# The embedding product moved to the start of a two-block network, with a new order of the queues around both places

## The reference

```python
h = rms_norm(x, norm_mix_pre);  z = h @ w_in            # nine splits: zq .. zu, zv, ga, gb
mix = merged(z) @ w_out;        x = x + rms_norm(mix, norm_mix_post)
h2 = rms_norm(x, norm_ffn_pre); ff = (silu(h2 @ w_gate) * (h2 @ w_up)) @ w_down
x = x + rms_norm(ff, norm_ffn_post)
x = x + (p @ w_ple) * sigmoid(x @ w_ple_gate)           # p: 256 x 256, w_ple: 256 x 1024
```

## Time and profile before

| What | us |
| --- | --- |
| median of 3 runs (1141.11 to 1141.41) | 1141.21 |
| the profiled execution | 1141.63 |
| its span, from first to last instruction | 1139.6 |
| PE busy | 1128.8 (99%) |
| DVE busy | 847.6 (74%) |
| ACT busy | 542.6 (48%) |
| first matmul of stage zu | 11.50 |
| first matmul of stage zv | 24.16 |

### The profile page before, as it was taken

One profiled execution on the slowest core, in us unless ns is written; L12 is line 12 of the kernel. 1 busy time (PEld: TensorE's weight loads), 2 busy tenths in 40 slices (PEclk: granted clock), 3 DMA queues, 4 the chain that ended last, 5 costly groups with the idle time before them and its releaser, 6 DMA issues.

```text
span 1139.6 us, 14114 instructions
## 1 busy us (share of the span) xinstructions
PE 1128.8 (99%) x5874; PEld 965.8 (85%) x5874; DVE 847.6 (74%) x951; ACT 542.6 (48%) x545; POOL 29.2 (3%) x51
## 2 busy tenths in 40 slices
PE   9999999999999999999999999999999999999997
PEld 7998998888888888888888888889988888888886
DVE  6789879977766768567676767579976866767685
ACT  6646556633753444355644444353333435444431
POOL 1000000000100000000000000000001000000000
PEclk9999999999999999999999999999999999999999
DMA  7854554447557787544467777558763664886760
GB/s 268 318 214 152 183 215 138 163 153 307 214 206 301 253 309 264 221 171 146 151 233 284 272 281 297 200 211 302 273 233 118 231 249 159 308 303 254 305 223 37
DMA packets 37534, 259.81 MB, mean 228 GB/s; under 512 B 4192, under 2 KB 4704, under 8 KB 6880
## 3 DMA queue, kind: packets, MB, share of 16 engines
q1 hardware_dynamic: 35856, 251.84, 59.7%
q0 software_dynamic: 1616, 7.08, 1.8%
HBM read 257.86 MB, written 1.05 MB: 227 GB/s over the span
## 4 chain that ended last, share of the span: by engine, by line
PE 96%; issue 1%; DVE 1%; ACT 1%; DMA 1%; SPq 0%; POOL 0%; POOLq 0%; DVEq 0%; ACTq 0%
PE pair L460 47%; PE pair L523 23%; PE pair L486 10%; PE pair L539 4%; PE tp L587 3%; PE tp L669 3%; PE tp L885 1%; PE pair L823 1%; PE tp L696 1%; DMA raw<-stream 1%; PE tp L861 1%; PE tp L610 0%; PE tp L649 0%; PE pair L728 0%; PE pair L722 0%
## 5 line engine op out<-in xcount | busy, mean ns | idle before, releaser
L1324 DVE TENSOR_TENSOR w_lo<-raw,w_hi 128x2048 fp32r<-128x2048 f32 x180 | 409.0, 2288 | 78.8 <-ACT w_hi L911 78.3
L911 ACT ACTIVATE w_hi<-raw 128x2048 fp32r<-128x2048 f32 x180 | 344.2, 1916 | 225.6 <-DMA raw<-stream 125.0
L460 PE MATMUL pair<-w_hi,ht_lo 128*128 128x512 f32 x800 | 316.3, 395 | 0.0
L460 PE MATMUL pair<-w_lo,ht_hi 128*128 128x512 f32 x800 | 311.9, 390 | 0.0
L460 PE MATMUL pair<-w_hi,ht_hi 128*128 128x512 f32 x800 | 311.6, 389 | 0.0
L460 PEld LDWEIGHTS pair<-w_lo,ht_hi 128*128 128x128 f32 x800 | 150.2, 188 | 31.7
L460 PEld LDWEIGHTS pair<-w_hi,ht_lo 128*128 128x128 f32 x800 | 150.3, 188 | 30.0 <-DVE ht_lo L1384 0.5
L460 PEld LDWEIGHTS pair<-w_hi,ht_hi 128*128 128x128 f32 x800 | 150.4, 188 | 29.5
L1333 DVE SCALAR_TENSOR_TENSOR raw<-raw,crow 128x1024 f32<-128x1024 f32 x112 | 132.3, 1219 | 0.9 <-DMA raw<-stream 0.9
L523 PE MATMUL pair<-w_hi,gt_lo 128*128 128x512 f32 x272 | 107.0, 393 | 0.3 <-DVE gt_lo L1400 0.3
L523 PE MATMUL pair<-w_lo,gt_hi 128*128 128x512 f32 x272 | 106.0, 390 | 0.0
(11 more groups left out here) (258 smaller groups left out, 1316.3 us busy)
## 6 DMA issues: line engine op xcount, KB each, us to landing
raw<-stream SPq DMA_DIRECT2D x237, 1024.0 KB, 4.9
xres<-x SPq DMA_DIRECT2D x2, 512.0 KB, 5.0
raw<-stream SPq DMA_DIRECT2D x4, 256.0 KB, 7.2
prow<-rows POOLq DMA_DIRECT2D x1, 1024.0 KB, 8.5
xres<-x POOLq DMA_DIRECT2D x2, 512.0 KB, 5.3
dt<-decay POOLq DMA_DIRECT2D x1, 1024.0 KB, 9.5
csr<-dft POOLq DMA_DIRECT2D x1, 768.0 KB, 6.2
sgw<-sg_wT POOLq DMA_DIRECT2D x1, 512.0 KB, 5.3
```

The lines of the kernel that those rows point to most:

```text
L460: mm = pe.matmul(pair[use % 2][:, t, :], a[:, 4 * c + k, t * P:(t + 1) * P], b[:, w % WS, k * 512:(k + 1) * 512], start=(c == 0 and k == 0 ...
L911: sc.activation(w_hi[:, w % WS, :], raw[:, n % RAW, :], ACT.Copy).then_inc(hi_done, 1)
L1324: v.tensor_tensor(w_lo[:, w % WS, :], raw[:, n % RAW, :], whi32[:, w % WS, :], ALU.subtract).then_inc(raw_done, 1)
```

## The change

Stage `ple` becomes the first of the stream. SP asks for p first, then for chunk 0 (now ple) and chunk 1 (now the first of zu) in four pieces each, and for chunk 2. x's two tiles, the identity and the table `col` are issued by ACT, with a semaphore each for the last two (`idn_in`, `col_in`). p lies in another place in memory, `plex` at the end, and the memory set aside for the descriptors of GpSimd's DMAs is given as 8192 bytes. The product goes in four quarters `embed(0..3)` into three free PSUM banks and one more, in front of and behind the first transposes; `keep_warm` goes, and WARM is 12. ACT's four copies are spread over the start. Every tick in the mixer moves by one, as do the numbers of the `ada` ticks there. Behind the mixer, PE has no `embed()`, and ACT and DVE have another order of ticks and norms. Cut to its core:

```diff
-WARM = 18
+WARM = 12
 RAW = 3
 WS = 4
 GROUPS = FT // 2
-STAGES = [("zu", 2), ("zv", 2), ("qa", 2), ("fa", 2), ("ba", 2), ("zi", 4), ("zg", 4),
+STAGES = [("ple", 1), ("zu", 2), ("zv", 2), ("qa", 2), ("fa", 2), ("ba", 2), ("zi", 4), ("zg", 4),
...
-FINE = 2
+FINE = 3
...
-        praw = sb("praw", 193.25, [P, 2, S])
-        pt = [sb("pt_hi", 195.25, [P, 2, S], F32R), sb("pt_lo", 197.25, [P, 2, S], F32R)]
+        praw = sb("praw", 112, [P, 2, S])
+        pt = [sb("pt_hi", 114, [P, 2, S], F32R), sb("pt_lo", 116, [P, 2, S], F32R)]
...
+        def embedding(t, half):
+
+            if t == 0:
+                return pair[1][:, half, :]
+            return tp[BANKS - 1][:] if half else pair[0][:, 1, :]
...
-            sp.dma_start(xres[:, 0, :], x[:, 0, :]).then_inc(x_in[0], 16)
-            sp.dma_start(idn[:], ident).then_inc(small_in, 16)
-            sp.dma_start(xres[:, 1, :], x[:, 1, :]).then_inc(x_in[1], 16)
-            sp.dma_start(col[:], cols).then_inc(small_in, 16)
+            def piece(n, q, sem):
+                part = slice(q * 512, (q + 1) * 512)
+                sp.dma_start(raw[:, n, part], stream[n][:, part]).then_inc(sem[q], 16)
+
+            sp.dma_start(praw[:], pT).then_inc(p_in, 16)
+            piece(0, 0, first_in)
+            piece(0, 1, first_in)
+            piece(0, 2, first_in)
+            piece(0, 3, first_in)
             for q in range(PIECES):
-                sp.dma_start(raw[:, 0, q * 512:(q + 1) * 512], stream[0][:, q * 512:(q + 1) * 512]).then_inc(first_in[q], 16)
-            for n in range(1, RAW):
-                sp.dma_start(raw[:, n, :], stream[n]).then_inc(landed[n], 16)
+                piece(1, q, next_in)
+            sp.dma_start(raw[:, 2, :], stream[2]).then_inc(landed[2], 16)
...
-            pool.wait_ge(merged, 2)
-            pool.dma_start(praw[:], pT).then_inc(p_in, 16)
...
+            def embed(q):
+
+                k, half = q // 2, q % 2
+                part = slice(q * 512, (q + 1) * 512)
+                for t in range(TT):
+                    out = embedding(t, half)
+                    tk = slice(t * P, (t + 1) * P)
+                    if t == 0:
+                        pe.wait_ge(hi_done, q + 1)
+                    pe.matmul(out, pt[0][:, k, tk], w_hi[:, 0, part], start=(k == 0), stop=False)
+                    if t == 0:
+                        pe.wait_ge(pt_done, 1)
+                    pe.matmul(out, pt[1][:, k, tk], w_hi[:, 0, part], start=False, stop=False)
+                    if t == 0:
+                        pe.wait_ge(raw_done, q + 1)
+                    mm = pe.matmul(out, pt[0][:, k, tk], w_lo[:, 0, part], start=False, stop=(k == 1))
+                if k == 1:
+                    mm.then_inc(ple_done, 1)
...
-            pe.wait_ge(small_in, 32)
+            def last_tile():
+                pe.wait_ge(ple_read, 2)
+                first_tile(1, 1, xn_done, 2)
+
+            pe.wait_ge(pt_hi, 1)
+            embed(0)
+            embed(1)
+            pe.wait_ge(idn_in, 16)
             first_tile(0, 0, xn_half, 1)
-            keep_warm(8)
-            first_part(0, 0, after={0: next_halves})
-            first_part(0, 1, after={1: lambda: first_tile(1, 1, xn_done, 2)})
+            embed(2)
+            embed(3)
+            pe.matmul(tp[1][:, 0:16], ones[:], ones[:, 0:16], start=True, stop=True).then_inc(w_used, 1)
+            first_part(0, 0, after={1: next_halves})
+            pe.wait_ge(ple_read, 1)
+            first_part(0, 1, after={3: last_tile})
             first_part(1, 0)
             first_part(1, 1)
+            pe.wait_ge(ple_read, 4)
...
-            embed()
...
+            act.dma_start(xres[:, 0, :], x[:, 0, :]).then_inc(x_in[0], 16)
+            act.dma_start(idn[:], ident).then_inc(idn_in, 16)
+            act.dma_start(col[:], cols).then_inc(col_in, 16)
+            act.dma_start(xres[:, 1, :], x[:, 1, :]).then_inc(x_in[1], 16)
...
+            def embedded(t, half):
+                act.wait_ge(ple_done, half + 1)
+                sc.activation(plex[:, t, half * 512:(half + 1) * 512], embedding(t, half), ACT.Copy).then_inc(ple_read, 1)
+
+            act.wait_ge(p_in, 16)
+            sc.activation(pt[0][:], praw[:], ACT.Copy).then_inc(pt_hi, 1)
+            hi_piece(0, 0)
             norm_squares(RQ["norm0"], 0, 0)
-            norm_squares(RQ["norm0"] + 1, 1, 0)
-            for q in range(2):
+            for q in range(1, PIECES):
                 hi_piece(0, q)
             norm_hi("norm0", 0, 0)
-            for q in range(2, PIECES):
-                hi_piece(0, q)
+            norm_squares(RQ["norm0"] + 1, 1, 0)
+            hi_piece(1, 0)
+            embedded(1, 0)
+            for q in range(1, PIECES):
+                hi_piece(1, q)
             first_scaled(0)
             norm_hi("norm0", 1, 0)
+            embedded(1, 1)
             for q in range(PIECES):
-                hi_piece(1, q)
+                hi_piece(2, q)
             norm_hi("norm0", 0, 1)
             first_scaled(1)
             norm_hi("norm0", 1, 1)
-            for w in range(2, WS):
-                split_hi(w)
+            embedded(0, 0)
+            embedded(0, 1)
+            split_hi(3)
+            tick(0)
             act.wait_ge(lb_e, 1)
             sc.activation(lbt[:, 1, :], lbt[:, 0, :], ACT.Exp).then_inc(lb_e, 1)
-            tick(0)
-            pair_ready(1)
+            tick(1)
...
             post_squares(RQ["mix"], 0, w + 3, USE["wout"], 3)
             tick(w)
             norm_squares(RQ["mix"] + 1, 0, 1)
-            act.wait_ge(p_in, 16)
-            sc.activation(pt[0][:], praw[:], ACT.Copy).then_inc(pt_hi, 1)
             tick(w + 1)
             for half in range(2):
                 norm_scaled("norm1", 0, colv("ffn_pre", 0, 8), None, hb[:, tile_job("norm1", 0, half) % 2, :], half)
                 norm_hi("norm1", 0, half)
+            tick(w + 2)
             post_squares(RQ["mix"] + 2, 1, w + 3, USE["wout"], 3)
-            embedded(0)
-            tick(w + 2)
             tick(w + 3)
             norm_squares(RQ["mix"] + 3, 1, 2)
-            for n in range(1, 4):
-                embedded(n)
-            tick(W0["ple"])
             norm_his("norm1", 1, colv("ffn_pre", 0, 8))
...
+            dve.wait_ge(pt_hi, 1)
+            v.tensor_tensor(pt[1][:], praw[:], as_f32(pt[0][:]), ALU.subtract).then_inc(pt_done, 1)
+            lo_piece(0, 0)
+            mean(RQ["norm0"])
+            lo_piece(0, 1)
+            dve.wait_ge(rstd_done, RQ["norm0"] + 1)
             first_norm(0, 0, xn_half)
             first_norm(0, 1, xn_done)
-            dve.wait_ge(small_in, 32)
+            lo_piece(0, 2)
+            dve.wait_ge(col_in, 16)
+            first_scaled(0)
+            lo_piece(0, 3)
+            norm_lo("norm0", 0, 0)
             mean(RQ["norm0"] + 1)
-            first_scaled(0)
+            lo_piece(1, 0)
             dve.wait_ge(rstd_done, RQ["norm0"] + 2)
             first_norm(1, 0, xn_half)
-            lo_piece(0, 0)
-            norm_lo("norm0", 0, 0)
             for q in range(1, PIECES):
-                lo_piece(0, q)
+                lo_piece(1, q)
             first_norm(1, 1, xn_done)
             norm_lo("norm0", 1, 0)
             first_scaled(1)
-            lo_piece(1, 0)
+            lo_piece(2, 0)
             norm_lo("norm0", 0, 1)
             for q in range(1, PIECES):
-                lo_piece(1, q)
+                lo_piece(2, q)
...
             post(RQ["mix"], 0, USE["wout"], prow[:, 0, :])
             mean(RQ["mix"] + 1)
-            dve.wait_ge(pt_hi, 1)
-            v.tensor_tensor(pt[1][:], praw[:], as_f32(pt[0][:]), ALU.subtract).then_inc(pt_done, 1)
             scale_norm(RQ["mix"] + 1, 0)
             tick(w)
             tick(w + 1)
             norm_lo("norm1", 0, 0)
             norm_lo("norm1", 0, 1)
+            tick(w + 2)
             dve.wait_ge(x_again[1], 16)
             post(RQ["mix"] + 2, 1, USE["wout"], prow[:, 0, :])
-            tick(w + 2)
+            tick(w + 3)
             mean(RQ["mix"] + 3)
-            tick(w + 3)
             scale_norm(RQ["mix"] + 3, 1)
-            tick(W0["ple"])
             norm_jobs("norm1", 1, colv("ffn_pre", 0, 8))
```

More of the change, by code:

```diff
@@ L127, in plan_psum @@
              ("offb", 2, "off_copied"), ("pvb", 2, "pv_read"), ("ta", 4, "split"),
-             ("tm", 4, "split"), ("norm1", 2, "norm"), ("ple", 4, "ple_read"), ("norm1b", 2, "norm"),
+             ("tm", 4, "split"), ("norm1", 4, "norm"),
              ("h0", GROUPS, "split"), ("tx", 4, "split"),
@@ L159, in tile_job @@
         return JOB[name] + 2 * half + t
-    return (JOB[name + "b"] if name in ("norm1", "norm2") and t else JOB[name] + 2 * t) + half
+    return (JOB[name + "b"] if name == "norm2" and t else JOB[name] + 2 * t) + half
 PIECES = 4
-FINE = 2
+FINE = 3
 def pieces_done(n):
@@ L282, in program @@
         first_in = [sem(f"first_in{q}") for q in range(PIECES)]
+        next_in = [sem(f"next_in{q}") for q in range(PIECES)]
```

(45 more changed lines are left out.)

30 lines of the change are left out of this document (14 added, 16 removed).

## The result

| | before | changed |
| --- | --- | --- |
| median, us | 1141.4 (1141.11 to 1141.54, 5 runs) | 1147.88 (1146.44 to 1147.95, 5 runs) |
| the profiled execution | 1141.63 | 1146.62 |
| its span | 1139.6 | 1144.4 |
| first matmul of zu | 11.50 | 15.14 |
| first matmul of zv | 24.16 | 30.86 |

The changed kernel is slower: ratio 1.0052, 95% interval 1.0041 to 1.0063. The prediction (1144.0, range to 1147.0) had the sign right and the size too small; the median lies 0.9 above its range. The single times stand apart in two groups: 1146.44 and 1146.62, then 1147.88, 1147.90 and 1147.95. The profile is of the lower group.

A forecast was written before the change was run, and what follows sets the result against it. PE was taken as the bound, holding 96% of the time. Start +4.9 and boundary -2.1 sum to +2.8; the profiled execution (1141.63) gives 1144.4, the median 0.4 lower, 1144.0, range 1139.6 to 1147.0.

The forecast's parts named there:

- Landings at the start: Estimated DMA landings: p 4.3, x's first tile 5.4, chunk 0's quarters 5.5, 6.8, 8.2, 9.2; 2 us either way possible.
- the term for the start: Start of the kernel: zv begins at 29.1 instead of 24.2, +4.9, range +3.9 to +6.
- Step 2 and 3: Start: PE through embedding, transposes and matmul on ones at 13.0; zu's first product at 13.6 instead of 11.50.
- step 4: ACT from 12.9 to chunk 3: 10.4 of work and 1.5 of waiting; chunk 3 starts there at 24.8.
- the wait of 1.6 for a low part: PE, through its work at 27.5, waits until 29.1 for DVE's low part of chunk 3 before zv.
- x's tile late: Rival at the start: x shares the rate, lands at 7.5 instead of 5.4, all slides by 1.5: 1145.5; chance 0.10.
- The sentence on landings 1 us later: Start: with every landing 1 us later, zv would start at 30.1 instead of 29.1.
- the case of the slow clock: Rival at the start: the embedding runs at 1.2 GHz, 4.8 more, 3.4 on the path: 1147.4; chance 0.05.
- The boundary: Behind the mixer: removing 5.57 of PE work gives -2.1, after waits of 0.8, 0.4 and 2.3; bounds 0 and -4.8.
- The rule weighed: At the start, two issuing queues share the same 16 DMA engines, so x's tile shares the rate; only issue time saved.
- The rival "faster": PE's idling before 11.5 takes the embedding whole; start costs 0 to 0.5, boundary gives 2.1 to 4.8: 1138; chance 0.10.
- the bound with no other limit: Start term if ACT and DVE were no limit: PE's own work from 6.2, about 18.4, making +0.5.

The follow-up runs named there:

- the two profiles named above: Changed kernel with 18 matmuls on ones (1146.62 to 1148.22), and changed kernel with ACT's last two embedding copies behind chunk 3's split (1146.54).
- one queue: Changed kernel with x's two tiles, the identity and the columns table issued by SP between chunk 0's quarters, nothing by ACT: 1146.02, ratio 1.0039.
- both: Changed kernel with SP alone loading x's first tile ahead of p, lists reordered, 16 matmuls on ones, and post and scaling ahead of chunks at the boundary: 1142.21.
- supply of quarters: The version called both, with identity and `col` issued by ACT, and x's second tile and its squares behind chunk 0's quarters: 1142.62, ratio 1.0011.
- the run with only this part: Kernel before without the embedding product and its weights, with the changed kernel's boundary order and descriptor memory: 1140.47, ratio 0.9991.
- The reordered one: Changed kernel with ACT's squares and DVE's post of tile 1 ahead of chunk w+2, mean and scaling ahead of tick(w+3): 1146.5, ratio 1.0042.

## Why the prediction was wrong

**What failed first is the part "Landings at the start": the term for the start was +4.9 and measured +6.7 at zv, +6.8 at the boundary.** I took p at 4.3, x's first tile at 5.4 and chunk 0's quarters at 5.5, 6.8 and so on. Measured: p 6.0, x's tile 6.2, the quarters that ACT waited for 7.0, 9.7 and 10.6. p and the first quarter stand ahead of x's squares on ACT, so these begin at 7.5 instead of 6.0, and all that follows is 1.5 later; the quarter alone would have done it, by the two profiles named above. This was within the "2 us either way" that I had written, but the range was made from landings 2 us earlier and only 1 us later (+3.9 to +6), so what I had called possible was cut off on the side where it came. Step 2 and 3 then slide whole: zu 15.14 for 13.6. The lists behind kept their lengths: my step 4 gave ACT 11.9 from 12.9 to chunk 3, and it took 12.0, from 14.47 to 26.48. Zv is at 30.86 for 29.1, and the wait of 1.6 for a low part is 1.63. So the mechanism of the start was right and its term mis-sized.

**The case "x's tile late" had the right slide for half the reason,** and 0.10: everything 1.5 later, 1145.5. It let x alone be late; here p and the first quarter were, and x by 0.8. Its row (x's tiles at a median of 5.0 and the quarters at 7.2) was a warning against landings of 3.6 for p and 4.3 for a quarter with more bytes asked for at once; behind that median stand 3.9 for the first tile, at the head of the queue, and 6.1 for the second. The run with one queue shows the other half: there p comes early and x late. Every order that was tried holds back something: x's first tile landed 5.5, 6.1, 4.4 and 5.0 behind its issue (changed kernel, one queue, both, supply of quarters), p 5.3, 2.6, 4.7 and 5.8, and the last two had zu's first product within 0.01 of each other.

**The sentence on landings 1 us later gave 30.1** for zv; 1.5 later is 30.6, and the measured 30.86 is 0.3 from it.

**The second thing that failed is the case of the slow clock: it had 0.05, and the clock fell, as far as times and profiles tell, in 7 of the 10 executions of the changed kernel.** I priced a late rise, all 24 products at 0.43. What happens is a fall behind a wait of 1.7 to 1.9, over some 8 matmuls, worth 1.4, and in some executions a second one behind the wait at the boundary, worth some 1.5. I had the matmuls on ones last until about 6.0 (they did, 6.36) and PE's first product at 6.2, so no hole behind them was in my list; it follows from the mis-sized landings. The wait of 2.3 at the boundary was in it, and I did not ask what the clock does behind that. Of the 3.9 between 1144.0 and the median, 1.3 is the median's distance to the profiled execution, which had no fall, 0.4 the one I had taken off for it, 1.9 the start (6.8 as seen at the boundary, for 4.9), -0.1 the boundary, 0.2 the time around the span (2.2 instead of 2.0), and some 0.2 is left. Without the fall the median would have been near 1146.5, within the range, with the start still mis-sized.

**The boundary was right.** Forecast -2.1 with waits of 0.8, 0.4 and 2.3; measured -2.2 with 0.80, at most 0.16, and 1.87, and -2.2 in the run with only this part. The reordered one shows that the two chunks ahead of `post` and scaling were the cause, and that a further 1.5 was there. The middle wait was put 0.2 too high and the last 0.4; that the sum is off by only 0.1 is in part luck, for each wait in brackets is some 0.16 shorter than the gap that it makes (a matmul is shown as 0.39 long, the next starts after 0.23).

**The rule weighed.** One queue gave p in 2.6, two queues in 4.6 to 5.3 (seven profiles). The Trainium skill, "DMA: Bandwidth & Descriptors", section "Issuing engines are not separate DMA queues", says just this, that transfers interleave whichever engine asked for them, and the run agrees with it. In the last experiment x's first tile landed 5.0 behind its issue, with 0.16 MB of small tables in the second queue, instead of 4.4 and 4.7 in the two versions with one queue; that points the same way, but the order of the weights differs too.

**The rival "faster"** failed where it was placed: ACT's list up to zu's first quarter, split at 14.47 and not by 11.5. What I had put at nothing beyond the start (late chunks, descriptor memory) came to 0.1: the distance to the kernel before is 6.7 at zv and 6.8 at the boundary.

**Two sums of the prediction are off by themselves.** PE's own work, 72 products and 12 transposes, is 17.7 by its unit prices and not 18.4, so the bound with no other limit is -0.3 and not +0.5; and 1141.2 - 4.8 is 1136.4, not 1136.6. Neither touches the forecast.

## What to carry to other kernels

Work moved into the idle start of a kernel is not free if it brings its own loads: list the bytes in order, and add them ahead of those on which the first useful product hangs. Ask first what lands latest, and which engine's list it blocks. A wait of the matmul engine of 1.7 to 1.9 us, as here, can cost twice, once itself and once by the clock behind it, in some executions and not in others; look at single times, not only at the median, and profile one of each group.

## What was not expected of the hardware

- Granted clock behind a wait: behind 12 matmuls on ones it fell to 0.5, for about 3 us, in the three profiles with waits of 1.69 to 1.90 and not in the two with 1.41 and 1.43; after a wait of 3.41, PE restarted at 0.5; in the last two versions, with 1.24 and 1.04 at the start and at most 0.80 at the boundary, none of 22 executions lies 1.4 above the others. Behind the wait of 1.87 at the boundary it fell in three profiles (0.50 to 0.61 in a stretch of 3 us, waits of 1.86 and 1.87) and not in five others (1.84 to 1.87), so there the length of the wait doesn't tell them apart.
- A POOL memset of `plex` held DVE up. In the kernel without the product it ran from 9.84 to 11.64, and DVE's scaling of x, elsewhere 0.48 long, took 1.59 and ended 0.3 behind it. DVE, then POOL:

```profile
10.33 1.59 DVE L1569 TENSOR_SCALAR xn<-xres,st 128x512 f32<-128x512 f32 x1
```

```profile
9.84 1.80 POOL L401 MEMSET plex<- 128x2048 f32 x1
```

  The Trainium skill, "SBUF — State Buffer", section "Who interferes with whom", has it that a DVE instruction in a two-port mode, which a `tensor_scalar` can take, contends with GpSimd for a shared pair of ports: the one issued first holds it for its whole length and the other waits. These rows agree; in which mode the scaling ran no row shows. Behind it PE waits 1.00 for a low part of DVE, and zv began 0.97 later than in the kernel before, at 25.14.
- Two small tables (64 and 100 KB) between the weights: from 6 to 9 us 276 GB/s passed with them in that queue (302 and 232 in two other versions), 370 with them in ACT's, 408 in the changed kernel. The order of the other loads differs between these as well, so that the tables are the cause isn't shown.
